# Splitting two more fp32 products of a decoder layer into high and low fp32r parts

## What is computed

```python
z = rmsnorm(x, norm_g) @ w_in        # columns: q_a k_a v_a g_a (1024 each), u_p g_p q_m g_m (512 each)
y_a = moba_attention(q_a, k_a, v_a) * silu(g_a)                # 8 heads of 128, causal
y_p = multiscale_pool(u_p, w_pool, pool_scale) * silu(g_p)     # 4 groups of 128 channels
y_m = memory_attention(q_m, mk, mv) * silu(g_m)                # 4 heads, 256 memory tokens
y = concatenate([y_a, y_p, y_m], axis=-1) @ w_out
return rmsnorm(x + y, final_norm_g)
```

## Time and profile before

| | |
|---|---|
| median of 3 runs | 428.13 us (428.09 to 428.76) |
| the profiled execution, its own time | 428.26 us |
| its span, first to last instruction | 426.5 us |
| TensorE busy | 417.3 us, 98% of the span |
| VectorE busy | 313.6 us, 74% |
| ScalarE busy | 249.5 us, 58% |
| GpSimd busy | 43.4 us, 10% |
| mean granted clock of TensorE | 0.997 |

### The profile page before, as it was taken

One profiled execution on the slowest core, in us unless ns is written; L12 is line 12 of the kernel. 1 busy time (PEld: TensorE's weight loads), 2 busy tenths in 40 slices (PEclk: granted clock), 3 DMA queues, 4 the chain that ended last, 5 costly groups with the idle time before them and its releaser, 6 DMA issues.

```text
span 426.5 us, 5775 instructions
## 1 busy us (share of the span) xinstructions
PE 417.3 (98%) x2184; PEld 357.9 (84%) x2184; DVE 313.6 (74%) x342; ACT 249.5 (58%) x335; POOL 43.4 (10%) x68
## 2 busy tenths in 40 slices
PE   8999999999999999999999999999999999999993
PEld 7888888888888888888888888888899888888882
DVE  4876888477987896856566778887667488897853
ACT  6764785257665667368465444755565566665611
POOL 1000003101001000000000341401000301000160
PEclk9999999999999999999999999999999999999998
DMA  8999739999599378955398256565646999467023
GB/s 285 415 414 421 315 105 303 297 412 320 146 386 271 129 25 328 421 226 197 100 116 243 62 184 202 192 199 167 228 148 223 247 405 275 186 246 295 3 87 110
DMA packets 29115, 99.48 MB, mean 233 GB/s; under 512 B 3872, under 2 KB 4384, under 8 KB 28192
## 3 DMA queue, kind: packets, MB, share of 16 engines
q1 hardware_dynamic: 24912, 84.31, 57.3%
q0 software_dynamic: 1728, 6.29, 8.0%
q10 hardware_dynamic: 2448, 8.52, 5.3%
HBM read 97.01 MB, written 2.10 MB: 232 GB/s over the span
## 4 chain that ended last, share of the span: by engine, by line
PE 91%; issue 3%; DVE 3%; DMA 1%; ACT 1%; DVEq 0%; POOLq 0%; POOL 0%; ACTq 0%
PE ps L660 29%; PE ps L663 14%; PE ps L719 4%; PE ps L717 4%; PE ps L718 4%; PE ps L676 4%; PE ps L678 4%; PE ps L677 4%; PE ps L702 4%; PE ps L700 4%; PE ps L701 4%; PE ps L641 3%; PE ps L648 1%; DMA mem_raw<-in_mem_head 1%; DVE x_f L1178 1%
## 5 line engine op out<-in xcount | busy, mean ns | idle before, releaser
L1167 DVE TENSOR_TENSOR w_lo<-w_raw,w_hi 128x1024 fp32r<-128x1024 f32 x131 | 163.3, 1263 | 61.5 <-ACT w_hi L916 60.6
L916 ACT ACTIVATE w_hi<-w_raw 128x1024 fp32r<-128x1024 f32 x131 | 135.9, 1056 | 64.7 <-PE ps L663 27.7
L660 PE MATMUL ps<-xT,w_hi 128*128 128x512 f32 x512 | 161.7, 397 | 0.0
L663 PEld LDWEIGHTS ps<-xT,w_lo 128*128 128x128 f32 x512 | 96.2, 188 | 22.7
L663 PE MATMUL ps<-xT,w_lo 128*128 128x256 f32 x512 | 100.6, 278 | 0.0
L660 PEld LDWEIGHTS ps<-xT,w_hi 128*128 128x128 f32 x512 | 78.3, 189 | 0.3
L717 PE MATMUL ps<-w_hi,xT 128*128 128x512 f32 x64 | 24.9, 389 | 0.0
L718 PE MATMUL ps<-w_lo,xT 128*128 128x512 f32 x64 | 24.9, 389 | 0.0
L719 PE MATMUL ps<-w_hi,xT 128*128 128x512 f32 x64 | 24.9, 389 | 0.0
L916 ACT ACTIVATE w_hi<-x_f 128x1024 fp32r<-128x1024 f32 x14 | 14.8, 1059 | 15.5 <-PE ps L719 10.1
L1167 DVE TENSOR_TENSOR w_lo<-x_f,w_hi 128x1024 fp32r<-128x1024 f32 x14 | 17.1, 1224 | 6.4 <-ACT w_hi L916 6.3
(11 more groups left out here) (220 smaller groups left out, 699.3 us busy)
## 6 DMA issues: line engine op xcount, KB each, us to landing
w_raw<-in_w_in SPq DMA_DIRECT2D x92, 512.0 KB, 6.7
w_raw<-in_w_out SPq DMA_DIRECT2D x30, 512.0 KB, 5.0
w_raw<-in_w_mem_kv SPq DMA_DIRECT2D x13, 512.0 KB, 12.2
x_f<-in_w_in SPq DMA_DIRECT2D x6, 512.0 KB, 7.1
x_f<-in_w_in POOLq DMA_DIRECT2D x6, 512.0 KB, 9.4
x_t_raw<-in_x_t SPq DMA_DIRECT2D x8, 256.0 KB, 12.9
rows<-in_x ACTq DMA_DIRECT2D x2, 1024.0 KB, 10.1
mem_rows<-in_mem ACTq DMA_DIRECT2D x2, 1024.0 KB, 10.2
```

The source lines that it names most:

```text
L660: pe.matmul(ps[:, bank0(g) + f, :], hi[:, t, f * P:(f + 1) * P], moving[:, kt], start=(kt == 0), stop=(kt == KT - 1), skip_group_check=True)
L663: m = pe.matmul(ps[:, bank0(g) + f, 0:S], lo[:, t, f * P:(f + 1) * P], moving[:, kt, 0], start=False, stop=(kt == KT - 1), skip_group_chec ...
L916: act.activation(halves_of(n)[0], whole_of(n), ACT.Copy).then_inc(hi_done, 1)
L1167: dve.tensor_tensor(lo, whole_of(n), hi.bitcast(F32), ALU.subtract).then_inc(lo_done, 1)
```

## The change

Two products get the three-part form. For the values: `v` over the first 128 keys is split once into `v_hi` and `v_lo` (group U, `a` = 2 on ScalarE, `a` = 3 on VectorE); `copy_probsT` writes `first_keys_hi` and, as a second copy, `second_keys`; VectorE's new `first_keys_low` subtracts. The second 128 keys stay one plain fp32 matmul. For the pool: the high parts of `w_pool` and of the pooled tokens are written by ScalarE at `a` = 2 of GP, the low parts by VectorE at `a` = 3 of GP, and TensorE waits for both low parts.

```diff
@@ weigh_values (TensorE) @@
+                else:
+                    pe.wait_ge(v_split, 1)
+                    pe.wait_ge(first_keys_split, 2 * JOBS.index(g) + pair + 1)
+                    pe.wait_ge(second_turned, 2 * JOBS.index(g) + pair + 1)
...
-                        pe.matmul(ps[:, b, 0:S], v[:, 0, c:c + HD], probsT[:, f, 0:S], start=True, stop=False)
-                        m = pe.matmul(ps[:, b, P:S], v[:, 1, c:c + HD], probsT[:, f, S:S + P],
-                                      start=False, stop=True)
+                        pe.matmul(ps[:, b, 0:S], v_hi[:, c:c + HD], first_keys_hi[:, f, :], start=True, stop=False)
+                        pe.matmul(ps[:, b, 0:S], v_hi[:, c:c + HD], first_keys_lo[:, f, :], start=False, stop=False)
+                        pe.matmul(ps[:, b, 0:S], v_lo[:, c:c + HD], first_keys_hi[:, f, :], start=False, stop=False)
+                        m = pe.matmul(ps[:, b, P:S], v[:, 1, c:c + HD], second_keys[:, f, :], start=False, stop=True)
@@ the mixing (TensorE) @@
-                    pe.wait_ge(wp_landed, 16)
-                    pe.wait_ge(pooled_ready, NF)
+                    pe.wait_ge(pool_split, 2)
                     for i in range(NF):
-                        m = pe.matmul(ps[:, bank0(g + 1) + i, 0:S], wp[:, i, :], u_pad[:, i, PAD:], start=True, stop=True)
+                        acc = ps[:, bank0(g + 1) + i, 0:S]
+                        pe.matmul(acc, wp_hi[:, i, :], pooled_hi[:, i, :], start=True, stop=False)
+                        pe.matmul(acc, wp_hi[:, i, :], pooled_lo[:, i, :], start=False, stop=False)
+                        m = pe.matmul(acc, wp_lo[:, i, :], pooled_hi[:, i, :], start=False, stop=True)
@@ copy_probsT (ScalarE) @@
+                if j >= 2:
+                    act.wait_ge(pv_done, j - 1)
+                act.activation(first_keys_hi[:, own, :], ps[:, b:b + 2, 0:S], ACT.Copy).then_inc(probsT_ready, 1)
+                act.activation(second_keys[:, own, :], ps[:, b:b + 2, S:S + P], ACT.Copy).then_inc(second_turned, 1)
@@ the loop over pieces (ScalarE) @@
+                if g == GP and a == 2:
+                    act.wait_ge(wp_landed, 16)
+                    act.wait_ge(pooled_ready, NF)
+                    act.activation(wp_hi[:, :, :], wp[:, :, :], ACT.Copy).then_inc(pool_hi_done, 1)
+                    act.activation(pooled_hi[:, :, :], u_pad[:, :, PAD:], ACT.Copy).then_inc(pool_hi_done, 1)
+                if g == U and a == 2:
+                    act.wait_ge(evacuated, V1 + 1)
+                    act.wait_ge(lo_done, unit_in(VP, N7, 1) + 1)
+                    act.activation(v_hi[:, :], v[:, 0, :], ACT.Copy).then_inc(v_hi_done, 1)
@@ first_keys_low, new (VectorE) @@
+                dve.wait_ge(probsT_ready, j + 1)
+                dve.wait_ge(second_turned, j + 1)
...
+                dve.tensor_tensor(first_keys_lo[:, own, :], ps[:, b:b + 2, 0:S], first_keys_hi[:, own, :].bitcast(F32),
+                                  ALU.subtract).then_inc(first_keys_split, 1)
@@ the loop over pieces (VectorE) @@
+                if g == GP and a == 3:
+                    dve.wait_ge(pool_hi_done, 2)
+                    low(wp_lo, wp, wp_hi).then_inc(pool_split, 1)
+                    low(pooled_lo, u_pad[:, :, PAD:], pooled_hi).then_inc(pool_split, 1)
...
+                if g == U and a == 3:
+                    dve.wait_ge(v_hi_done, 1)
+                    dve.tensor_tensor(v_lo[:, :], v[:, 0, :], v_hi[:, :].bitcast(F32), ALU.subtract).then_inc(v_split, 1)
+                if g in CAUSAL_JOBS and a == 4 + int(g == GA0):
+                    first_keys_low(g, 0)
+                    first_keys_low(g, 1)
```

More of the change, by code:

```diff
@@ L146, in build @@
         u_pad = sb("u_pad", [P, NF, PAD + S], F32, early)
+        first_keys_lo = sb("first_keys_lo", [P, NF, S], F32R, early)
         early.close()
@@ L149, in build @@
         mem_rows = sb("mem_rows", [P, TH, D], F32, early)
+        v_hi = sb("v_hi", [P, 2 * COLS], F32R, early)
+        v_lo = sb("v_lo", [P, 2 * COLS], F32R, early)
         early.close()
@@ L199, in build @@
         probs = sb("probs", [P, NF, 2 * S], F32, early)
-        probsT = sb("probsT", [P, NF, 2 * S], F32, early)
+        first_keys_hi = sb("first_keys_hi", [P, NF, S], F32R, early)
+        second_keys = sb("second_keys", [P, NF, P], F32, early)
         early.close()
@@ L205, in build @@
         sum_b = sb("sum_b", [P, NF, PAD + S], F32, early)
+        early.close()
+        early = ExitStack()
+        pooled_hi = sb("pooled_hi", [P, NF, S], F32R, early)
+        pooled_lo = sb("pooled_lo", [P, NF, S], F32R, early)
+        wp_hi = sb("wp_hi", [P, NF, P], F32R, early)
+        wp_lo = sb("wp_lo", [P, NF, P], F32R, early)
         early.close()
@@ L310, in build @@
         pooled_ready = sem("pooled_ready")
+        pool_hi_done = sem("pool_hi_done")
+        pool_split = sem("pool_split")
+        v_hi_done = sem("v_hi_done")
+        second_turned = sem("second_turned")
+        v_split = sem("v_split")
+        first_keys_split = sem("first_keys_split")
         mixed = sem("mixed")
@@ L968, in copy_probsT @@
                 act.wait_ge(probs_turned, j + 1)
-                w = 2 * S if g == MEM_JOB else S + P
                 b = bank0(g + 1) + 2 * pair
-                dst = (mem_probsT_hi if g == MEM_JOB else probsT)[:, 2 * pair:2 * pair + 2]
-                act.activation(dst[:, :, 0:w], ps[:, b:b + 2, 0:w], ACT.Copy).then_inc(probsT_ready, 1)
+                own = slice(2 * pair, 2 * pair + 2)
+                if g == MEM_JOB:
+                    act.activation(mem_probsT_hi[:, own, :], ps[:, b:b + 2, :], ACT.Copy).then_inc(probsT_ready, 1)
+                    return
+                if j >= 2:
+                    act.wait_ge(pv_done, j - 1)
+                act.activation(first_keys_hi[:, own, :], ps[:, b:b + 2, 0:S], ACT.Copy).then_inc(probsT_ready, 1)
+                act.activation(second_keys[:, own, :], ps[:, b:b + 2, S:S + P], ACT.Copy).then_inc(second_turned, 1)
             def copy_att(g, pair):
@@ L1349, in turned_lo, with first_keys_low @@
                                   ALU.subtract).then_inc(mem_probsT_split, 1)
+            def first_keys_low(g, pair):
+                j = 2 * JOBS.index(g) + pair
+                dve.wait_ge(probsT_ready, j + 1)
+                dve.wait_ge(second_turned, j + 1)
+                if j >= 2:
+                    dve.wait_ge(pv_done, j - 1)
+                own = slice(2 * pair, 2 * pair + 2)
+                b = bank0(g + 1) + 2 * pair
+                dve.tensor_tensor(first_keys_lo[:, own, :], ps[:, b:b + 2, 0:S], first_keys_hi[:, own, :].bitcast(F32),
+                                  ALU.subtract).then_inc(first_keys_split, 1)
             def window_sums():
```

## The result

The changed kernel takes 434.77 us (median of 5 runs, 433.37 to 435.27) against 428.18 us: 1.4% slower, ratio 1.014 with a 95% interval of 1.0129 to 1.0151. The time lies inside the predicted range, 2.3 us above the point forecast. Its profiled execution took 433.37 us and has a span of 431.6 us, 5.1 us more than the span before.

What follows compares the result with a forecast made beforehand. TensorE, busy 98% of the span, was taken to bound the kernel. Values -0.6, wait +5.3 and mixing -0.3 gave +4.4 on 428.26 us, so 432.7, or 432.5 us against the median; range 431.6 to 435.2.

Steps and rivals of the forecast that it cites:

- TensorE's savings: Three-part matmuls save 0.6 us on eight causal heads in U and GA0 and 0.3 us on GP's mixing.
- The covers of U and GA0: The values' new splits finish before TensorE asks, costing nothing; margins in GA0 0.9 and 1.4 us.
- The wait at the mixing: In GP TensorE stands ready at 274.5 and waits 5.3 us for VectorE's pooled_lo; bounds 5.0 to 6.1 us.
- The chain itself: VectorE's fixed order from the window sums at 236.24 to the end of pooled_lo at 280.06, before shifting.
- Its start: The window sums, waiting through GpSimd for the norm factors' broadcast, start 0.3 us earlier, by U's saving.
- the wait at the mixing with the clock kept: First case: TensorE waits before GP's mixing and stays at 2.4 GHz; 432.5 us, chance 0.50.
- the fall of the clock: Rival: TensorE's clock falls to 1.2 GHz in the wait before GP's mixing; 434.0 us, chance 0.33.
- The price: Coming up from the lower clock costs 1.5 us behind GP's wait, read from 22 passes at the kernel's start.
- the work costs by its amount: Rival raised with the experiments: ScalarE's and VectorE's added work costs wherever it stands; no chance given.
- the values bring a wait: Rival: a late ScalarE copy makes TensorE wait for first_keys_split in GA0; at most 433.5 us, chance 0.04.
- the change does not do what it says: Rival: the three-part matmuls run no faster than plain ones; 0.9 us more, 433.4 us, chance 0.02.
- that rival: GP's gate chain comes earlier through ScalarE's changed order, shortening the mixing's wait; 429.5 to 432 us, chance 0.06.

Runs made afterwards that it cites:

- e1: Changed kernel with the pool's mixing back to plain fp32 on all three engines, only the values in three parts: 427.52 us against 428.17 before.
- e3: Changed kernel with the pool's high and low parts moved to piece 1 of GP, low parts behind the gate's multiplication: 427.36 us against 428.17 before.
- e5: Changed kernel with all pool splits still written but TensorE mixing the unsplit operands in plain fp32: 427.50 us against 428.24 before.
- e4: Changed kernel with 20 filling matmuls ahead of TensorE's wait for the pool's low parts: 432.86 us against 428.17 before.
- e6: Changed kernel with the pool's low parts one place earlier on VectorE, piece 2 of GP, ahead of mk_lo: 427.93 us against 428.24 before.
- e10: Changed kernel with the edit of e9 plus 25 filling matmuls ahead of the wait for the pool's low parts: 433.09 us against 428.29 before.
- e7: Changed kernel with the broadcast of the memory's norm factors issued two pieces earlier in GA0: 433.50 us against 428.24 before.
- e2: Changed kernel with the causal values back to plain matmuls, only the pool's mixing in three parts: 433.62 us against 428.17 before.
- e11: The changed kernel unedited, measured again beside e10 on one chip: 432.95 us against 428.29 before.
- e8: Changed kernel with GpSimd clearing the pads ahead of its scaling of the memory keys: 434.31 us against 428.39 before.
- e9: Changed kernel with mv_lo moved ahead of the pool's two low parts on VectorE: 434.84 us against 428.39 before.

## Why the prediction was right, and which terms were off

**TensorE's savings: right.** 0.58 us a head as worked out, 0.6 us for the values (e1: 0.65). For the pool the three-part form alone is worth e3 less e1, 427.36 against 427.52: 0.16 us where 0.29 was worked out, inside the spread of either. The traces are closer: from the first matmul of the mixing to the last of the kernel it is 143.68 us in e1 and e5 with the plain form, and 143.40 to 143.50 in e3, e4, e6 and e10 with three parts.

**The covers of U and GA0: right.** Margins of 0.9 us for the first pair in GA0 were forecast; there was no wait in the changed kernel. e7 shows how thin it is: one GpSimd instruction beside VectorE turned it into 1.34 us of waiting.

**The wait at the mixing: right in kind and place, the size a little over.** Forecast 5.3 us; counted in the same way, from the moment when TensorE could go on, the profiled execution has 4.8 (4.6 of them idle). The chain itself was right to 0.01 us; it took 43.8 us in e2 and e11 too, and 44.3 in e7. Its start moved by 0.95 us and not by 0.3, because the broadcast was issued 0.4 us earlier and landed 0.6 us sooner after its issue than in the execution of before. The prediction took one landing time for a fixed one.

**The clock: the wrong case was put first.** The forecast was "the wait at the mixing with the clock kept", 0.50, and the fall of the clock had 0.33. In every profiled execution of this change with a wait of 3 us or more that was not filled (the changed kernel twice, e2, e7, e8, e9) the clock fell. The step that was off is the weighing of one row: behind the last matmul of the kernel before the clock fell after 4.7 us, and the prediction took that for the length that a pause needs. By that row itself a pause of 5.1 us would have been long enough, so even then the fall should have come first. And it is only one case. In these six executions the fall came 2.7 us (e8) to 4.8 us (e9) after the last matmul ahead of the pause, 4.0 us in the changed kernel's first; in e2 and e11 the matmuls had already gone on when it came.

The price had been worked out from the durations at the start of the kernel as 1.5 us, an estimate, since the trace lists a granted clock of 1.00 there. It was 1.3 us here and 1.6 us in e2, e7 and e11, with one low stretch of 3.4 us each, and 2.3 in e8 and 2.5 in e9, where the low stretch was 6.8 us long. These are the distances from the first matmul of the mixing to the last of the kernel (144.73, 145.04, 145.02, 145.04, 145.73, 145.99 us) less the 143.45 us of the executions without a fall.

The rule of the Trainium skill, "TensorE: Matmul & The Clock Gate", section "HAM oscillation — how this bites in real kernels", is that a pause between bursts takes the clock down and the burst behind it starts cold. These traces agree about the fall for the waits of 3 us and more, and not for the 1.2 us of e6. They agree about the cold start in four of the six: in e2 and e11 the first matmuls behind the pause stood 0.23 and 0.22 us, then 0.12 us apart, at full speed.

**Why 434.77 and not 433.4.** The profiled execution is the fastest of its five. The run of 435.27 us has a mean clock of 0.987, as e8 and e9 have with their longer low stretch. But the runs of 434.77 and 434.81 us have 0.993, the same as the profiled one, which speaks for a later landing there. They have no traces, and how the 1.4 us divide is open. So is what made the first median 1.8 us higher than that of e11, with the kernel before at 428.2 to 428.4 us beside every one of them. The clock's part in the medians is open too; its price is shown in the traces alone.

How near the forecast came owes something to luck: a wait that was 0.5 us too long and a fall of the clock that was left out, 1.3 us, partly cancel, and e11's median, 0.5 us above the forecast, looks better than the terms behind it were.

**The rivals.** That the work costs by its amount fell with e3 and e5, that the values bring a wait with e1. That the change does not do what it says fell with the timeline. The chain did come 0.65 us earlier than forecast, but by the broadcast and not by ScalarE's order, as that rival had it: VectorE's idle time before the split is 2.08 us as before.

## What to carry to other kernels

When a product is changed to need one more operand, find the instruction that writes that operand in its engine's fixed order, add up the chain in front of it from the trace, and compare its end with the moment the consumer arrives: here 2 us of VectorE's free work in the wrong place cost 4.7 to 6.6 us, and the same work two pieces of code earlier gained 0.8. A wait in a dense stream of matmuls can cost more than itself: here the waits of 3 to 6 us cost 1.3 to 2.5 us more by the clock, and the one of 1.2 us nothing more. A chain that begins with a small DMA inherits the spread of its landing, and one trace shows only one value of it.

## What the runs showed of the hardware that was not expected

- The clock can fall after a pause is over: in e2 TensorE had been issuing matmuls at full speed for 1.2 us behind a pause of 3.3 us when the granted clock went to 1.2 GHz, and in e11 for 0.3 us behind one of 4.1 us. A wait of 1.2 us (e6) left it alone.
- Beside GpSimd's scaling of 1024 columns, a VectorE instruction with both operands in SBUF took 3.42 us (e7) and 3.35 us (e8) in place of 1.2: in both cases it ended 1.1 us after GpSimd's did (229.26 against 228.17, 236.45 against 235.36), as if it had run behind it. Starting the instruction 2.2 us earlier in e8 gained nothing.
- GpSimd took up the same small broadcast, issued in the same place of the program, between 3.9 us (e1) and 6.8 us (the kernel before) after its issue.
